# Conditioning bias added by the tensor engine as a 12-row matmul, with the weight, decay-rate and input loads put in another order

## The chip, the cores and the metric

The kernel runs on one core of one Trainium2 chip. The metric is the device time of one execution in microseconds (us), as the median of several runs. TensorE is called PE here, its weight loads PEld, VectorE DVE, ScalarE ACT, GpSimd POOL and SyncE SP. A number such as L939 is a line of the kernel before.

## The reference

One decoder layer for 1024 prompt tokens and 8 single tokens of a decode batch. Only its beginning matters here: the conditioning vector `c` (9 rows: one for the prompt, eight for the samples) goes through one weight of 1024 x 6144, the bias is added, and the first two of six pieces scale and shift the normalised input before the input projection.

```python
def ada_mod(c, w, b):
    m = jax.nn.silu(c) @ w + b
    return m.reshape(c.shape[0], N_MOD, 1, D_MODEL)

def modulate(x, shift, scale):
    return layer_norm(x) * (1.0 + scale) + shift
...
        mp = ada_mod(c_prompt, w_ada[l], b_ada[l])
        ms = ada_mod(c_sample, w_ada[l], b_ada[l])
...
        op, stp = mixer(modulate(xp, mp[:, 0], mp[:, 1]), ...)   # proj = u @ w_in, then two head groups
...
        vp = modulate(xp, mp[:, 3], mp[:, 4])                    # then a top-2 mixture of 32 experts
```

The other pieces of the conditioning are a gate after each sub-layer and the second shift and scale. Behind the projection come a convolution, a recurrence and a scan, an output projection, and a mixture of experts.

## The kernel before

**Stages.** Each engine has its own program, written out by hand in order, and they meet only at semaphores; nothing is scheduled. The first stage (0 to about 73 us) does, on PE: transposes of `c` (L871) and of the eight normalised tiles of x (L885, function `x_turn`), of the eight sample rows (L909) and of small parameter rows (L914, 42 rows; L918, 29 rows). Then the conditioning for shift and scale comes in four pairs, `ada_pair(0)` to `ada_pair(3)`: each is 32 matmuls of a 128 x 32 stationary slice of `c` against a 128 x 128 piece of the weight (L895), four of them side by side in the four column groups of 32, and one transpose (L902). Then the projection begins: `project_split` (L939) runs 72 matmuls for each tile of 128 output columns, eight k slices of nine. For the first tile it waits slice by slice, and takes `ada_pair(2)` and `ada_pair(3)` before slices 2 and 4.

**What DVE and ACT do there.** DVE takes the statistics of each tile of x (L1132, `x_stats`) and normalises it (L1141, `x_norm`), copies the parameter rows out of PSUM (L1158, L1160) and halves some of them (L1161, L1162; PE's `ada_pair(0)` waits for L1162). For a pair it adds the bias (L1176, `u_pair`), copies the transposed result (L1178), applies scale and shift to two slices (L1184), and subtracts for the low part of the split into high and low parts (L1192, `u_low`), after ACT has cast the high part (L721). `w_high` (ACT, L713) and `w_low` (DVE, L1154) do the same for a tile of projection weights. `lam_rates` (DVE, L1100 to L1125) is a chain of 17 small instructions for the decay rates, which are used only much later.

**Late conditioning.** The remaining four pieces are computed between projection tiles: after each of the first eight tiles PE does two k steps, `ada` (L877), each of 4 matmuls with 512 columns, one in each column group. Steps 0 to 7 fill bank 6 of PSUM, steps 8 to 15 bank 7. DVE adds the bias when a bank is full (L1246, `mod_out`).

**Loads.** SP and ACT each issue four of the eight 512 KB tiles of x, even ones on SP behind the two loads of `c`, odd ones on ACT. POOL issues the bias, replicated over partitions in eight DMAs (`bada4` and `badaP`, L513 and L517), then the sample rows and the parameter rows.

Of the kernel before, what the change touches and what calls it, by code (L numbers as in the profile page):

```python
# [25 lines left out]
ALU = mybir.AluOpType  # L26
# [3 lines left out]
P = 128  # L30
# [50 lines left out]
def build_step(nc, x_prompt, x_sample, c_prompt, c_sample, state_lru_conv, state_lru_h, state_ssd_conv,  # L81
# [13 lines left out]
    with ctx:  # L95
# [95 lines left out]
        bada4 = sb("bada4", [P, 3, 512], scope=first)  # L191
        lnst = sb("lnst", [P, 2, 16], scope=first)
# [16 lines left out]
        modP, badaP = at(46300, 4, P), at(43904, 4, P)  # L209
# [71 lines left out]
        bada_ready = sem("bada_ready")  # L281
        sample_ready = sem("sample_ready")
# [104 lines left out]
        with nc.Block() as block:  # L387
            @block.sync
            def _(sp):
# [12 lines left out]
                for t in range(0, NT, 2):  # L402
                    sp.dma_start(xt[t], x_prompt[0, t * P:(t + 1) * P, :]).then_inc(xt_loaded[t], 16)
# [9 lines left out]
                load_pair(2)  # L413
                load_w(COL_XBC + P, 1)
                load_pair(3)
# [87 lines left out]
            def _(gp):  # L503
# [8 lines left out]
                for g in range(4):  # L512
                    gp.dma_start(bada4[32 * g:32 * g + 32, :, :],  # L513
                                 b_ada.rearrange("a (r g n) -> g a r n", r=3, g=4)[g].to_broadcast([32, 3, 512]))\
                        .then_inc(bada_loaded, 16)
                for g in range(4):
                    gp.dma_start(badaP[32 * g:32 * g + 32, :, :],  # L517
                                 b_ada[:, 0:2 * D].rearrange("a (s c i n) -> s i a c n", s=2, c=4, i=2)[g // 2, g % 2]
                                 .to_broadcast([32, 4, P])).then_inc(bada_loaded, 16)
# [8 lines left out]
                for dst, src in ((prow2[0:4, :], ssd_conv_w[0]), (prow2[4:5, :], ssd_conv_b),  # L528
                                 (prow2[5:29, :], state_ssd_conv[0].rearrange("b k n -> (b k) n"))):
                    gp.dma_start(dst, src).then_inc(rows2_loaded, 16)  # L530
                step(gp.memset(ones[:, :], 1.0))
# [126 lines left out]
            def _(act):  # L658
                step = Chain(act, ac)

                for t in range(1, NT, 2):
# [54 lines left out]
                for k in range(KT):  # L716
                    if k == 5:
                        w_high(1, 0)
                    act.wait_ge(u_ready, k + 1)
                    act.wait_ge(sample_ready, k // 2 + 1)  # L720
                    act.activation(us[:, 0, k, :], uT[:, k, :], ACT.Copy).then_inc(uh_ready, 1)  # L721
                act.wait_ge(small_loaded, 64)
# [142 lines left out]
            def _(pe):  # L865
# [8 lines left out]

                def ada(bank, k, w):
                    for g in range(4):
                        mm = pe.matmul(PS[32 * g:32 * g + 32, bank, :], cT[:, k, :], w[:, 512 * g:512 * g + 512],  # L877
                                       start=(k == 0), stop=(k == KT - 1))
                    return mm
# [9 lines left out]
                def ada_pair(c):  # L889
                    pe.wait_ge(pair_loaded[c], 32)  # L890
                    if c > 1:
                        pe.wait_ge(mod0_ready, c - 1)
                    for k in range(KT):
                        for g in range(4):
                            mm = pe.matmul(PS[32 * g:32 * g + 32, 6 + c % 2, 0:P], cT[:, k, :],  # L895
                                           pair[c][g // 2][:, k, P * (g % 2):P * (g % 2) + P],
                                           start=(k == 0), stop=(k == KT - 1))
# [22 lines left out]
                pe.wait_ge(vector_once, PT_READY)  # L920
                ada_pair(0)
# [172 lines left out]
            def _(ve):  # L1094
# [72 lines left out]
                ve.wait_ge(bada_loaded, 128)  # L1167
                step(ve.tensor_scalar(badaP[64:128, :, :], badaP[64:128, :, :], 1.0, None, ALU.add))
                step(ve.tensor_scalar(bada4[0:64, 2, :], bada4[0:64, 2, :], 1.0, None, ALU.add))
# [4 lines left out]
                def u_pair(c):  # L1174
                    ve.wait_ge(ada_mm, c + 1)
                    ve.tensor_tensor(modP[:, c, :], PS[:, 6 + c % 2, 0:P], badaP[:, c, :], ALU.add).then_inc(mod0_ready, 1)  # L1176
# [24 lines left out]
                lam_rates()  # L1201
# [4 lines left out]
                w_low(1, 0)  # L1206
                u_low(6)
                u_low(7)

# [24 lines left out]
                ve.tensor_tensor(wdts[:, 1, :, :], wdt[:, :, :], wdts[:, 0, :, :], ALU.subtract).then_inc(ul_ready, 1)  # L1234

# [1475 lines left out]
```

## Time and profile before

| | |
|---|---|
| median of 3 runs | 1527.1 us (1524.56 to 1530.54) |
| the profiled execution, its own time | 1527.24 us |
| its span in the trace | 1525.3 us |
| PE busy | 1360.6 us, 89% |
| DVE busy | 952.6 us, 62% |
| ACT busy | 572.0 us, 37% |
| POOL busy | 295.9 us, 19% |

The span is the stretch that the trace covers; the execution's own time is 1.9 us longer. Busy time of PE counts overlapping matmuls once, and their ends are modelled, so the start of the next instruction says more than the end of the last. The four parts of the program follow each other: the conditioning and the input (to 73 us), projection, scan and recurrence (to about 620 us), output projection and routing (to 913 us), the experts and the end.

### The profile page before, as it was taken

What the parts mean: (1) busy time and instruction counts of PE and PEld (TensorE: products, weight loads), DVE (VectorE), ACT (ScalarE), POOL (GpSimd) and SP (SyncE); (2) the same over time, 40 slices, a digit from 0 to 9 for tenths busy, and PEclk for the clock granted to TensorE, in tenths of its full rate; (3) what the DMA queues carried; (4) which work ended last, traced back from release to release, by engine and by line L of the source; (5) the groups of instructions that cost most, each with busy time, mean ns of one, the idle gap of its engine ahead of it and who ended that gap; (6) DMA issues with size and microseconds to landing.
All of it is one profiled execution on the core that took longest, in us unless ns stands there. A gap on an engine that the chain in (4) does not pass through costs nothing.

```text
span 1525.3 us, 38250 instructions
## 1 busy us (share of the span) xinstructions
PE 1360.6 (89%) x13487; PEld 1005.5 (66%) x13487; DVE 952.6 (62%) x1702; ACT 572.0 (37%) x886; POOL 295.9 (19%) x325
## 2 busy tenths in 40 slices
PE   4799999999999999789999449998899899999944
PEld 3689989899888888578588435544455455555521
DVE  5755553968999989876777565544444353351639
ACT  3322332535555665722232103433343243241522
POOL 4000002211000000200000013333333343443400
PEclk8899999999999999899999769999999999999977
DMA  9666415644334335832232949999999989978684
GB/s 284 194 241 238 155 42 160 212 147 141 113 113 123 116 113 190 307 96 96 75 99 77 391 161 404 407 406 407 408 407 398 407 349 354 407 290 335 242 334 154
DMA packets 169586, 365.87 MB, mean 240 GB/s; under 512 B 16040, under 2 KB 94944, under 8 KB 166312
## 3 DMA queue, kind: packets, MB, share of 16 engines
q1 hardware_dynamic: 150616, 308.72, 55.2%
q0 software_dynamic: 18320, 54.08, 10.1%
q10 hardware_dynamic: 576, 2.10, 0.4%
q8 instruction: 45, 0.74, 0.2%
q14 instruction: 29, 0.24, 0.0%
HBM read 324.06 MB, written 45.63 MB: 242 GB/s over the span
## 4 chain that ended last, share of the span: by engine, by line
PE 29%; DMA 19%; DVE 7%; issue 2%; SPq 1%; ACT 0%; DVEq 0%; POOLq 0%; ACTq 0%
DMA ring<-in_w_down_dram 18%; PE PS L2069 10%; PE PS L2200 8%; PE PS L2218 5%; DVE big L2270 1%; PE PS L2188 1%; PE PS L2100 1%; DMA ring<-in_w_up_dram 1%; PE PS L2135 1%; PE PS L2209 1%; DVE ring L2647 1%; DVE ring L2652 1%; PE PS L2092 1%; DVE ring L2661 1%; SPq L1678 1%
## 5 line engine op out<-in xcount | busy, mean ns | idle before, releaser
L939 PE MATMUL PS<-big 128*128 128x344 f32 x2592 | 423.0, 323 | 1.7 <-DVE big L1192 1.7
L939 PEld LDWEIGHTS PS<-big 128*128 128x128 f32 x2592 | 411.9, 189 | 10.4 <-issue 6.7
L2200 PE MATMUL PS<-ring,arena 128*32 128x256 f32 x5248 | 301.0, 381 | 0.5 <-DVE arena L2537 0.5
L2200 PEld LDWEIGHTS PS<-ring,arena 128*32 128x32 f32 x5248 | 162.1, 110 | 114.2 <-issue 15.0
L2218 PE MATMUL PS<-ring,arena 128*32 128x256 f32 x2624 | 165.1, 394 | 21.9 <-DVE arena L2545 21.9
L1833 POOL DMA_INDIRECT arena<-v_d,icur x84 | 103.2, 1229 | 281.3 <-DVE icur L2549 159.1
L2000 ACT ACTIVATE ring<-ring 128x1024 f32 x124 | 121.0, 1047 | 58.8 <-PE PS L2200 58.0
L2218 PEld LDWEIGHTS PS<-ring,arena 128*32 128x32 f32 x2624 | 78.7, 112 | 78.4 <-DVE arena L2545 23.7
L1841 POOL DMA_INDIRECT f_d<-arena,scur x82 | 105.8, 1290 | 65.5 <-issue 45.0
L2541 DVE SCALAR_TENSOR_TENSOR arena<-arena,PS 128x128 f32<-128x128 f32 x82 | 23.6, 288 | 138.6 <-ACT arena L1977 93.3
L2592 DVE COPY ring<-ring 128x4096 f32 x31 | 72.7, 2345 | 55.9 <-SPq L1712 41.3
L2537 DVE COPY arena<-PS 128x256 f32<-128x256 f32 x82 | 34.7, 423 | 99.4 <-PE PS L2188 97.8
L1972 ACT ACTIVATE arena<-PS 128x256 f32<-128x256 f32 x82 | 30.7, 374 | 166.5 <-PE PS L2200 166.5
L2069 PE MATMUL PS<-low 128*128 128x512 f32 x256 | 83.3, 407 | 10.9 <-issue 5.0
L1982 ACT ACTIVATE arena<-PS 128x256 f32<-128x256 f32 x82 | 31.4, 383 | 151.0 <-PE PS L2218 151.0
L2579 DVE COPY ring<-ring 128x1024 f32 x124 | 80.3, 688 | 9.2 <-PE PS L2200 3.6
L2069 PE MATMUL PS<-big,low 128*128 128x512 f32 x256 | 81.0, 398 | 0.0
L2069 PE MATMUL PS<-low,big 128*128 128x512 f32 x256 | 80.9, 398 | 0.0
L2069 PEld LDWEIGHTS PS<-low 128*128 128x128 f32 x256 | 47.2, 193 | 22.0 <-issue 8.2
L1154 DVE TENSOR_TENSOR big<-arena,big 128x1024 fp32r<-128x1024 f32 x20 | 24.5, 1225 | 55.4 <-ACT big L713 55.3
L2069 PEld LDWEIGHTS PS<-low,big 128*128 128x128 f32 x256 | 49.3, 193 | 10.9
L2069 PEld LDWEIGHTS PS<-big,low 128*128 128x128 f32 x256 | 49.2, 192 | 10.8
(469 smaller groups left out, 1833.3 us busy)
## 6 DMA issues: line engine op xcount, KB each, us to landing
ring<-in_w_gate_dram SPq DMA_DIRECT2D x32, 2048.0 KB, 10.5
ring<-in_w_up_dram SPq DMA_DIRECT2D x32, 2048.0 KB, 15.6
ring<-in_w_down_dram SPq DMA_DIRECT2D x32, 2048.0 KB, 8.6
arena<-in_w_ada_dram SPq DMA_DIRECT2D x16, 1024.0 KB, 6.8
arena<-in_w_in_dram SPq DMA_DIRECT2D x20, 512.0 KB, 8.0
upper<-in_w_ada_dram SPq DMA_DIRECT2D x8, 1024.0 KB, 11.6
upper<-in_w_in_dram SPq DMA_DIRECT2D x16, 512.0 KB, 4.0
arena<-acs_d SPq DMA_DIRECT2D x8, 1024.0 KB, 4.8
```

Source lines behind the costliest of these rows:

```text
L939: mm = pe.matmul(PS[:, 3 * b + a, 0:CU], wss[b][:, i, k, :], us[:, j, k, a * CU:(a + 1) * CU], start=(k == 0 and (i, j) == PARTS[0]), stop ...
L1833: gp.indirect_dma_start(xg[b], None, v_q, bass.IndirectOffsetOnAxis(ap=icur[b][:, :], axis=0), bounds_check=QW * (SEQ + DEC) - 1, oob_is_e ...
L1841: gp.indirect_dma_start(f_q, bass.IndirectOffsetOnAxis(ap=scur[b][:, :], axis=0), yo[b], None, bounds_check=QW * 2 * (SEQ + DEC) - 1, oob_ ...
L1972: act.activation(hb, PS[:, 3, 0:FH], ACT.Copy).then_inc(hb_ready, 1)
L1982: act.activation(yo[b], PS[:, 6, 0:DQ], ACT.Copy).then_inc(yo_ready, 1)
L2000: act.activation(wcur[:, 1024 * q:1024 * q + 1024], ring[:, bass.ds(w + 1024 * q, 1024)], ACT.Copy).then_inc(gate_copied, 1)
L2069: mm = pe.matmul(PS[:, bank + n, :], (yh[h % 2], yl3[h % 3])[a][:, k, :], (WH, WL)[b][i][:, 512 * n:512 * n + 512], start=(k == 0 and (a, ...
L2200: mm = pe.matmul(PS[32 * g:32 * g + 32, 3, 0:FH], xT[:, c, CAP * q:CAP * q + CAP], wcur[:, w:w + FH], start=(q == 0 and c == 0), stop=(q = ...
L2218: mm = pe.matmul(PS[32 * g:32 * g + 32, 6, 0:DQ], hT[:, c % 2, CAP * (c // 2):CAP * (c // 2) + CAP], wcur[:, 8192 + 1024 * c + DQ * g:8192 ...
L2537: ve.tensor_copy(xT, PS[:, 0, 0:2 * P].rearrange("p (c t) -> p c t", c=2)).then_inc(xT_ready, 1)
L2579: ve.tensor_copy(wcur[:, 4096 + 1024 * q:5120 + 1024 * q], ring[:, bass.ds(w + (4096 + 1024 * q), 1024)]).then_inc(up_copied, 1)
L2592: ve.tensor_copy(wcur[:, GU:GU + DN], ring[:, bass.ds(w, DN)]).then_inc(down_copied, 1)
```

## The change

The bias is loaded once as 12 rows of 512 columns (`brow`, chunk r in partition r), in one DMA in place of eight. POOL builds a column that is 1 in rows 2, 3, 8 and 9 (the two scales) from the identity, and DVE adds it to the 12 rows; PE's first pair now waits for that (`bada_ready`). Each accumulation of the conditioning then begins with a matmul of 12 partitions, whose stationary operand is one column of the identity broadcast to 32 columns, so that it puts row `chunk` of the bias in all 32 output rows. DVE's two additions of the bias become copies. The remaining edits move things: the order of x over the two queues, the second tile of projection weights behind the fourth pair of weights, its cast behind the eight slices on ACT and its subtraction behind them on DVE, and `lam_rates` behind the last of that on DVE.

```diff
-                for t in range(0, NT, 2):
+                for t in (2, 4, 6, 7):
                     sp.dma_start(xt[t], x_prompt[0, t * P:(t + 1) * P, :]).then_inc(xt_loaded[t], 16)
...
                 load_pair(2)
+                load_pair(3)
                 load_w(COL_XBC + P, 1)
-                load_pair(3)
...
-                for g in range(4):
-                    gp.dma_start(bada4[32 * g:32 * g + 32, :, :],
-                                 b_ada.rearrange("a (r g n) -> g a r n", r=3, g=4)[g].to_broadcast([32, 3, 512]))\
-                        .then_inc(bada_loaded, 16)
-                for g in range(4):
-                    gp.dma_start(badaP[32 * g:32 * g + 32, :, :],
-                                 b_ada[:, 0:2 * D].rearrange("a (s c i n) -> s i a c n", s=2, c=4, i=2)[g // 2, g % 2]
-                                 .to_broadcast([32, 4, P])).then_inc(bada_loaded, 16)
+                gp.dma_start(brow, b_ada.rearrange("a (r n) -> (a r) n", n=512)).then_inc(bada_loaded, 16)
...
+                step(gp.tensor_tensor(scale_row[0:NB_ADA, 0:2], ident[0:NB_ADA, 2:4], ident[0:NB_ADA, 8:10], ALU.add))
+                gp.tensor_tensor(scale_row[0:NB_ADA, 2:3], scale_row[0:NB_ADA, 0:1], scale_row[0:NB_ADA, 1:2], ALU.add)\
+                    .then_inc(scale_row_made, 1)
...
-                for t in range(1, NT, 2):
+                for t in (0, 1, 3, 5):
                     act.dma_start(xt[t], x_prompt[0, t * P:(t + 1) * P, :]).then_inc(xt_loaded[t], 16)
...
                 for k in range(KT):
-                    if k == 5:
-                        w_high(1, 0)
                     act.wait_ge(u_ready, k + 1)
                     act.wait_ge(sample_ready, k // 2 + 1)
                     act.activation(us[:, 0, k, :], uT[:, k, :], ACT.Copy).then_inc(uh_ready, 1)
+                w_high(1, 0)
...
+                def bias(out, chunk, lo, n):
+                    pe.matmul(out, ident[0:NB_ADA, chunk:chunk + 1].to_broadcast([NB_ADA, 32]), brow[:, lo:lo + n],
+                              start=True, stop=False)
+
                 def ada(bank, k, w):
                     for g in range(4):
+                        if k == 0:
+                            bias(PS[32 * g:32 * g + 32, bank, :], 4 * (bank - 5) + g, 0, 512)
                         mm = pe.matmul(PS[32 * g:32 * g + 32, bank, :], cT[:, k, :], w[:, 512 * g:512 * g + 512],
-                                       start=(k == 0), stop=(k == KT - 1))
+                                       start=False, stop=(k == KT - 1))
...
+                    for g in range(4):
+                        bias(PS[32 * g:32 * g + 32, 6 + c % 2, 0:P], 2 * (g // 2) + c // 2, 256 * (c % 2) + P * (g % 2), P)
...
                 pe.wait_ge(vector_once, PT_READY)
+                pe.wait_ge(bada_ready, 1)
                 ada_pair(0)
...
-                ve.wait_ge(bada_loaded, 128)
-                step(ve.tensor_scalar(badaP[64:128, :, :], badaP[64:128, :, :], 1.0, None, ALU.add))
-                step(ve.tensor_scalar(bada4[0:64, 2, :], bada4[0:64, 2, :], 1.0, None, ALU.add))
+                ve.wait_ge(bada_loaded, 16)
+                ve.wait_ge(scale_row_made, 1)
+                ve.tensor_scalar(brow, brow, scale_row[0:NB_ADA, 2:3], None, ALU.add).then_inc(bada_ready, 1)
...
-                    ve.tensor_tensor(modP[:, c, :], PS[:, 6 + c % 2, 0:P], badaP[:, c, :], ALU.add).then_inc(mod0_ready, 1)
+                    ve.tensor_copy(modP[:, c, :], PS[:, 6 + c % 2, 0:P]).then_inc(mod0_ready, 1)
...
                 u_low(3)
-                lam_rates()
                 u_pair(2)
                 u_low(4)
                 u_low(5)
                 u_pair(3)
-                w_low(1, 0)
                 u_low(6)
                 u_low(7)
+                w_low(1, 0)
...
                 ve.tensor_tensor(wdts[:, 1, :, :], wdt[:, :, :], wdts[:, 0, :, :], ALU.subtract).then_inc(ul_ready, 1)
+                lam_rates()
...
-                    ve.tensor_tensor(modS[r], PS[:, 5 + r, :], bada4[:, r, :], ALU.add).then_inc(mod_ready, 1)
+                    ve.tensor_copy(modS[r], PS[:, 5 + r, :]).then_inc(mod_ready, 1)
```

On PE, the end of the first projection tile and the two late steps behind it read so before (L939 is the projection, L877 the late step; a row counts matmuls of one kind in a row):

```order
L939 MATMUL PS<-big 128x344 x18
L895 MATMUL PS<-upper 32x128 x32
L902 MATMUL PS<-ident,upper 128x128
L939 MATMUL PS<-big 128x344 x36
L877 MATMUL PS<-arena,upper 32x512 x8
L939 MATMUL PS<-big 128x344 x72
```

and so in the changed kernel, where L948 is the projection, L903 the pair, L876 the bias and L883 the late step:

```order
L948 MATMUL PS<-big 128x344 x18
L876 MATMUL PS<-bada,ident 32x128 x4
L903 MATMUL PS<-upper 32x128 x32
L910 MATMUL PS<-ident,upper 128x128
L948 MATMUL PS<-big 128x344 x36
L876 MATMUL PS<-bada,ident 32x512
L883 MATMUL PS<-arena,upper 32x512
L876 MATMUL PS<-bada,ident 32x512
L883 MATMUL PS<-arena,upper 32x512
L876 MATMUL PS<-bada,ident 32x512
L883 MATMUL PS<-arena,upper 32x512
```

In a pair the four bias matmuls stand together ahead of the 32; in a late bank each of them stands alone, in turn with one matmul of the first k step. The same alternation comes once more, at the first step of the second bank, behind the fifth projection tile.

On DVE, the last two pairs up to the projection loop read so before (L1176 is the bias added to a pair, L1192 `u_low`, L1154 `w_low`, L1100 the beginning of `lam_rates`, which goes on to L1125):

```order
L1100 TENSOR_SCALAR sm<-sm 128x8
...
L1125 TENSOR_SCALAR spl<-sm 128x8
L1176 TENSOR_TENSOR upper<-PS,upper 128x128
...
L1184 TENSOR_SCALAR arena<-arena,ssT 128x1024
L1154 TENSOR_TENSOR big<-arena,big 128x1024
L1192 TENSOR_TENSOR big<-arena,big 128x1032 x2
L1234 TENSOR_TENSOR wdts<-wdt,wdts 128x128
```

and so in the changed kernel (L1185 the copy of a pair, L1201 `u_low`, L1163 `w_low`, L1109 to L1134 `lam_rates`):

```order
L1185 COPY upper<-PS 128x128
...
L1201 TENSOR_TENSOR big<-arena,big 128x1032 x2
L1163 TENSOR_TENSOR big<-arena,big 128x1024
L1242 TENSOR_TENSOR wdts<-wdt,wdts 128x128
L1109 TENSOR_SCALAR sm<-sm 128x8
...
L1134 TENSOR_SCALAR spl<-sm 128x8
```

`lam_rates` has gone from ahead of the third pair to behind everything that the first projection tile needs, and `w_low` from ahead of the last two `u_low` to behind them.

## Rows read from the trace of the kernel before

**Rows 1.** Busy us of each engine in two stretches, then granted PE clock, DMA share, GB/s.

```profile
39.00:54.50 15.50, 12.11 (x148) 10.47 (x148) 10.99 (x21) 5.20 (x6) 0.00 (x0) 0.64 1.10 361
...
130.00:500.00 370.00, 357.69 (x2388) 332.10 (x2388) 270.49 (x432) 160.72 (x235) 36.10 (x50) 1.00 0.44 140
```

**Rows 2.** Timeline at the start, DVE: start, length, instruction, idle before and releaser.

```profile
10.88 1.29 DVE L1132 BATCH_NORM_STATS2 lnst<-arena 128x6 f32<-128x512 f32 x2 [1.88 <-DMA arena<-in_x_prompt_dram]
...
16.30 1.29 DVE L1132 BATCH_NORM_STATS2 lnst<-arena 128x6 f32<-128x512 f32 x2 [1.14 <-DMA arena<-in_x_prompt_dram]
```

**Rows 3.** ACT's tiles of x, issue to landing; then each queue's packets, MB, share.

```profile
L662 ACTq DMA_DIRECT2D arena<-in_x_prompt_dram x4: 395/456/497, 0.9 to 2.3; - x4
...
DMA to landing us min/median/max: 3.9/6.7/9.5
...
q10 hardware_dynamic: 478, 1.76, 42.4%
q1 hardware_dynamic: 239, 0.88, 22.5%
...
q1 hardware_dynamic: 854, 2.40, 38.7%
```

**Rows 4.** Timeline from the parameter rows to the second pair.

```profile
38.95 3.64 PE L895 MATMUL PS<-upper 128*32 128x128 f32 x64 [0.99 <-DVE PT L1162]
...
39.21 0.42 DVE L1168 TENSOR_SCALAR upper<-upper 64x512 f32<-64x512 f32 x1
...
49.75 0.33 PE L902 MATMUL PS<-ident,upper 128*128 128x128 f32 x1 [2.48 <-DVE upper L1176]
```

**Rows 5.** Timeline around the third pair.

```profile
54.50 1.96 PE L895 MATMUL PS<-upper 128*32 128x128 f32 x64
54.95 0.17 DVE L1100 TENSOR_SCALAR sm<-sm 128x8 f32<-128x8 f32 x1
...
58.22 0.29 DVE L1176 TENSOR_TENSOR upper<-PS,upper 128x128 f32<-128x128 f32 x1
```

**Rows 6.** Timeline around the fourth pair and the last slices.

```profile
61.65 1.95 PE L895 MATMUL PS<-upper 128*32 128x128 f32 x64
...
63.36 1.23 DVE L1192 TENSOR_TENSOR big<-arena,big 128x1032 fp32r<-128x1032 f32 x1 [0.67 <-ACT big L721]
64.51 0.28 DVE L1176 TENSOR_TENSOR upper<-PS,upper 128x128 f32<-128x128 f32 x1
...
66.65 2.02 ACT L721 ACTIVATE big<-arena 128x1032 fp32r<-128x1032 f32 x2 [3.32 <-DVE arena L1188]
67.19 1.22 DVE L1154 TENSOR_TENSOR big<-arena,big 128x1024 fp32r<-128x1024 f32 x1
68.33 2.37 DVE L1192 TENSOR_TENSOR big<-arena,big 128x1032 fp32r<-128x1032 f32 x2
...
69.71 3.06 PE L939 MATMUL PS<-big 128*128 128x344 f32 x18 [1.68 <-DVE big L1192]
```

**Rows 7.** Timeline of the first late steps, and what PE and DVE do behind.

```profile
72.70 1.92 PE L877 MATMUL PS<-arena,upper 128*32 128x512 f32 x16
...
73.95 1.23 DVE L1154 TENSOR_TENSOR big<-arena,big 128x1024 fp32r<-128x1024 f32 x1 [3.05 <-ACT big L713]
74.55 11.35 PEld L939 LDWEIGHTS PS<-big 128*128 128x128 f32 x72 [0.84 <-issue]
```

**Rows 8.** PE's groups by shape: busy us, mean ns of one; idle before.

```profile
L877 PE MATMUL PS<-arena,upper 128*32 128x512 f32 x80 | 9.6, 598 | 0.0
```

**Rows 9.** Timeline where PE's shape changes (stationary 8, then 42 partitions), and where not.

```profile
34.53 1.02 PE L909 MATMUL PS<-ident,arena 8*128 8x8 f32 x8
...
35.48 1.08 PE L914 MATMUL PS<-ident,arena 42*128 42x42 f32 x8
...
410.42 1.03 PE L1038 MATMUL PS<-ident,arena 128*128 128x128 f32 x8
411.21 9.08 PE L939 MATMUL PS<-big 128*128 128x344 f32 x56
```

More of the change, by code:

```diff
@@ L191, in build_step @@
         bada4 = sb("bada4", [P, 3, 512], scope=first)
+        scale_row = sb("scale_row", [P, 3], scope=first)
         lnst = sb("lnst", [P, 2, 16], scope=first)
@@ L208, in build_step @@
         modS = [None] + [at(o, 512) for o in (46300, 23176)]
-        modP, badaP = at(46300, 4, P), at(43904, 4, P)
+        modP = at(46300, 4, P)
+        NB_ADA = 12
+        brow = bada4[0:NB_ADA, 0, :]
         xb2 = [at(A0 + 1060 * b, 1060) for b in range(2)]
@@ L281, in build_step @@
         bada_ready = sem("bada_ready")
+        scale_row_made = sem("scale_row_made")
         sample_ready = sem("sample_ready")
@@ L530, in _ @@
                     gp.dma_start(dst, src).then_inc(rows2_loaded, 16)
+                gp.wait_ge(gpsimd_once, IDENT_MADE)
+                step(gp.tensor_tensor(scale_row[0:NB_ADA, 0:2], ident[0:NB_ADA, 2:4], ident[0:NB_ADA, 8:10], ALU.add))
+                gp.tensor_tensor(scale_row[0:NB_ADA, 2:3], scale_row[0:NB_ADA, 0:1], scale_row[0:NB_ADA, 1:2], ALU.add)\
+                    .then_inc(scale_row_made, 1)
                 step(gp.memset(ones[:, :], 1.0))
@@ L896, in ada_pair @@
                                            pair[c][g // 2][:, k, P * (g % 2):P * (g % 2) + P],
-                                           start=(k == 0), stop=(k == KT - 1))
+                                           start=False, stop=(k == KT - 1))
                     mm.then_inc(ada_mm, 1)
```

## The prediction

> **What bounds the kernel now.** I read the windows first. From 130 to 500 us PE is busy for 357.69 of 370 us while DVE has 270 and ACT 161 [rows 1]: behind the first stage the core is bound by PE, and every later stage is started by semaphores that come from there. So an edit to the first 75 us is worth what it does to the moment when PE gets to the second projection tile, and whatever it adds to PE behind that moment counts in full. The timeline of the first stage then shows four places where PE doesn't set the pace:
>
> - DVE's chain of statistics and normalising waits 1.88 us for the first tile of x and 1.14 us for the third [rows 2]; later tiles are there when it comes.
> - `ada_pair(0)` starts at 38.95, released by DVE [rows 4]. It takes 3.64 us for what the third pair does in 1.96 [rows 4, 5]: the granted clock is 0.64 on average from 39 to 54.5 us [rows 1], that is, partly at 1.2 and partly at 2.4 GHz.
> - The third pair ends at 56.46, but DVE takes its result only at 58.22, since the 17 instructions of `lam_rates` stand between (from 54.95) [rows 5].
> - Behind the fourth pair DVE's `w_low` (67.19) stands ahead of `u_low`, which PE's last two slices wait for: 1.68 us at 69.71 [rows 6].
>
> **The change part by part.** A minus sign is a gain.
>
> *Order of x.* ACT's first tile lands 3.9 us after an issue at 0.93, that is at 4.8; its second and third within 6.7 and 9.5 us of issues up to 2.3, by 9.0 and 11.8; SP's first is the one that released DVE at 10.88 [rows 2, 3]. In the new order DVE has tile 0 when it comes, at 9.0 (10.88 less its wait), tile 1 (wanted 1.4 later, at 10.4) from ACT's second slot, and tile 2 (wanted at 16.30 less 1.14 less 1.88 = 13.3) from SP's first. The last ones come on SP in its third and fourth slot; SP's queue has moved 2.40 MB by 22 us, more than the 2.1 MB of its x [rows 3], and they are wanted near 22.6 and 24.9 (tiles follow each other at 2.3 us). So both waits go: **-3.02**. The eight bias DMAs also leave POOL's queue, 1 MB of traffic in the same stretch; I count nothing for it, since nothing is left to wait.
>
> *The 12 rows.* The load, the two POOL instructions and the DMAs behind them are tens of us early. But PE's first pair now also waits for DVE's addition to the 12 rows, which stands where L1168 stood: 39.21, and as long, 0.42 (512 elements per partition in both), so it ends at 39.63. Before, PE began at 38.95, 0.05 or so behind the instruction that released it; now that is 39.68: **+0.73**. Behind PE's wait only the pairs are queued, and DVE has nothing else to do until the first one ends.
>
> *Bias in the pairs.* Four matmuls more per pair are an eighth of a pair: 0.45 at the low clock, 0.25 at the high one. They have 12 partitions where the pair has 128, so PE's shape changes in between. Where the stationary operand goes from 8 to 42 partitions, the next matmul begins 0.07 us before the end of the last (34.53 + 1.02 against 35.48), whereas between two groups of 128 x 128 it begins 0.24 before (410.42 + 1.03 against 411.21) [rows 9]. A change of shape thus loses the overlap of one matmul with the next, 0.17 us at most. I take 0.6 for the first pair and 0.4 for the third and fourth. The second pair ends well ahead of DVE (PE waits 2.48 us behind it [rows 4]): nothing. First pair: **+0.6**.
>
> *lam_rates moved.* DVE can now take the third pair when PE has it, 56.46 + 0.15 = 56.6 in place of 58.22: **-1.6**, and PE's 0.4 is in the path there: **+0.4**. In its new place `lam_rates` fills the 3.05 us in which DVE waits before 73.95 [rows 7]; its 3.3 us may push the next `w_low` by some tenths, but PE needs that one only a tile (11 us) later, so even without the gap it would cost PE nothing until those 11 us were used up.
>
> *w_high and w_low moved.* Without `w_high` in between, ACT has slice 5 cast earlier and DVE loses its wait of 0.67 at 63.36; it could take the fourth pair at 63.84, PE has it at 61.65 + 1.95 + 0.15 = 63.75 plus 0.4 = 64.15, in place of 64.51: **-0.36**. Then `u_low(6)` begins when ACT's first cast is done (66.65 + 1.01, so 67.7) in place of 68.33: **-0.6** for PE's slices 6 and 7 [rows 6]. The moved `w_low` and its load behind `load_pair(3)` are wanted only after the late steps, some 3 us later. The swap on SP's queue brings the fourth pair earlier and the tile later, both with more than 10 us in hand.
>
> Up to the end of the first projection tile: -3.02 + 0.73 + 0.6 - 1.6 + 0.4 - 0.36 - 0.6 = **-3.9**.
>
> *Bias in the late banks.* Here the four bias matmuls aren't together. Each stands between matmuls of 128 partitions, so there are seven changes of shape and seven stretches in which only one column group works, where before four did. A matmul of fp32 is two instructions in the trace (16 for two steps of four). In its 1.92 us [rows 7] there are four rounds of four side by side, so one round streams (1.92 - 0.60) / 3 = 0.44, with 0.60 for one instruction [rows 8]. One matmul by itself: 0.44 + 0.60 - 0.07 (the overlap left at a change) = 0.97. Seven of them, with the eighth overlapping the second step as before: 6.8 us. This falls into PE's own stream, at the end of tile 0 (PE runs from 72.70 to 74.55 without a gap of its own [rows 7]) and again at the end of tile 4. Two banks: **+13.6**.
>
> Here a rule of the Trainium skill bears on the change: TensorEngine Tiling (Array Packing), under Tiling Modes, Key Properties, says that changing the tiling mode, and not just the tile, drains the engine, and lists 32, 64 and 128 rows as modes. The trace agrees (0.07 against 0.24, [rows 9]); by it alone one would get the same 0.97 for each stretch, and without it the first rival below.
>
> DVE's copies in place of additions have the same size and the same single PSUM source; the late one is off the path. Nothing.
>
> **Sum.** -3.9 + 13.6 = +9.7. Against the profiled execution: 1527.24 + 9.7 = 1536.9; the median of the runs is 0.1 lower than that execution, so 1536.8.
>
> **Rivals.**
>
> 1. *The shape doesn't matter: not slower.* If bias matmuls overlap with their neighbours as the four column groups do now, a bank's bias costs two rounds, 0.88, not 6.8, and a pair's 0.45 or 0.25. Then -3.02 + 0.73 + 0.45 - 1.6 + 0.25 - 0.5 - 0.6 + 1.76 = -2.5, 1524.6. For it: the column groups stay the same, and [rows 9] show only groups with other work between semaphores. Against: the overlap left is 0.07 there. It decides below 1.9 us per bank. Chance 0.15.
> 2. *The low clock.* If PE falls to 1.2 GHz in one of the stretches with a single column group (it does twice in the first 55 us), its seven streams of 0.88 double: +6, 1543. For it: less of the array works. Against: by the records PE is hardly idle there, and from 100 us on it stays at full clock [rows 1]. Chance 0.1. The low stretches before 55 us may also shift; the first pair is worth 1.7 us (3.64 against 1.96) either way.
> 3. *x comes later than its slot says.* ACT's queue has moved 1.76 MB by 12 us and SP's 0.88 [rows 3]. Were they even in the new order (1.3 MB each), ACT's second tile would be complete near 10 us and usable 1.5 us after it is wanted: -1.5 in place of -3.0, 1538.3. Chance 0.06. The Trainium skill says in DMA: Bandwidth & Descriptors, Queues, rings and completion order, that each DMA engine serves its queues in turn; the trace doesn't show even shares in this stretch.
> 4. *The delay is taken up later*, by DVE's or the DMA's own waits: some 1530. Against: PE has 12 us of idle time in 370 [rows 1], and what waits for it shifts with it. Chance 0.03.
>
> **How the numbers follow.** The forecast has 0.66, with 1533.5 to 1540.5 as its own range (a tenth of the 0.97 either way is 1.4 us, the first pair's clock 1.7, the x order 1.5). To leave out no more than 2 in 10, the range takes rivals 3 and 4 and most of 2: 1530 to 1543.5; what is left out is above all rival 1. About 0.5% (7.6 us) is what a measurement of this kernel can tell from no change: faster is below 1519.5, for which no case stands, 0.01; slower is above 1534.7, with nearly nine tenths of the forecast and rivals 2 and 3, 0.75; the rest 0.24.
>
> **What would show it.** In the trace of the changed kernel: statistics of the first tile at 9.0 and no wait at the third (x); the first pair near 36.7, released by the addition to the 12 rows; DVE at the third pair at 55.3 in place of 58.22 (`lam_rates`); slice 6 near 65.8; and between the first tile and the second, PE's late steps near 8.7 us long in place of 1.85, with bias and weight matmuls in turn, one per 0.97 us. The second tile's first matmul would then be at 74.55 + 2.9 = 77.5. If the late steps take under 3 us, rival 1 holds and the forecast is wrong; if a single one takes 1.4 us or more, it is the clock.

## The result, and the profile after

The changed kernel takes **1542.24 us** (median of 6 runs, 1538.09 to 1543.38), against 1529.4 us for the kernel before in the same series (6 runs, 1524.56 to 1533.06). The ratio on record is 1.0078, 95% interval 1.0061 to 1.0096: 11.9 us slower (9.3 to 14.7). The two medians differ by 12.8; here and below the ratios on record are used, which differ a little from the quotients of the medians. The profiled execution took 1542.43 us, with a span of 1540.8. The forecast was 1536.8, in a range of 1530 to 1543.5.

PE's timeline of the changed kernel from the last slices of the first projection tile to the start of the second (start, length, instruction, count; idle before and releaser in brackets). It answers to [rows 6] and [rows 7], and its end is the second pass through late steps, at the end of tile 4:

```profile
62.14 3.06 PE L948 MATMUL PS<-big 128*128 128x344 f32 x18 [1.10 <-DVE big L1201]
65.13 1.04 PE L876 MATMUL PS<-bada,ident 12*32 12x512 f32 x2
66.10 1.05 PE L883 MATMUL PS<-arena,upper 128*32 128x512 f32 x2
67.08 1.04 PE L876 MATMUL PS<-bada,ident 12*32 12x512 f32 x2
68.05 1.04 PE L883 MATMUL PS<-arena,upper 128*32 128x512 f32 x2
69.02 1.04 PE L876 MATMUL PS<-bada,ident 12*32 12x512 f32 x2
69.99 1.05 PE L883 MATMUL PS<-arena,upper 128*32 128x512 f32 x2
70.97 1.04 PE L876 MATMUL PS<-bada,ident 12*32 12x512 f32 x2
71.94 1.90 PE L883 MATMUL PS<-arena,upper 128*32 128x512 f32 x10
73.77 4.52 PE L948 MATMUL PS<-big 128*128 128x344 f32 x27
...
125.56 1.04 PE L876 MATMUL PS<-bada,ident 12*32 12x512 f32 x2
...
132.37 1.90 PE L883 MATMUL PS<-arena,upper 128*32 128x512 f32 x10
134.21 11.01 PE L948 MATMUL PS<-big 128*128 128x344 f32 x68
```

The single row of [rows 7] (72.70, 1.92 us, 16 instructions) has become eight rows. None has an idle time in brackets, and still each starts 0.97 us behind the one before. Two steps that took 74.55 - 72.70 = 1.85 us now take 73.77 - 65.13 = 8.64 us, and at tile 4 again 134.21 - 125.56 = 8.65. PE counts as busy all the time: nothing in the chain of waits or in the idle columns shows this loss. It shows in starts that follow each other by 0.97 us, where four matmuls side by side used to stream in 0.44 (the prediction's working from [rows 7] and [rows 8]).

The first stage, where the change moves work, from the timeline of the changed kernel (it answers to [rows 2] and [rows 4 to 6]):

```profile
8.69 1.27 DVE L1141 BATCH_NORM_STATS2 lnst<-arena 128x6 f32<-128x512 f32 x2
...
10.12 1.23 DVE L1141 BATCH_NORM_STATS2 lnst<-arena 128x6 f32<-128x512 f32 x2
...
33.05 0.19 DVE L1171 TENSOR_SCALAR PT<-PT 128x60 f32<-128x60 f32 x1
33.43 0.47 DVE L1178 TENSOR_SCALAR bada<-bada,scale_row 12x512 f32<-12x512 f32 x1
34.00 0.42 PE L876 MATMUL PS<-bada,ident 12*32 12x128 f32 x8 [1.70 <-DVE sm L1174]
34.35 3.21 PE L903 MATMUL PS<-upper 128*32 128x128 f32 x64
...
49.32 0.42 PE L876 MATMUL PS<-bada,ident 12*32 12x128 f32 x8
49.67 1.95 PE L903 MATMUL PS<-upper 128*32 128x128 f32 x64
51.69 0.29 DVE L1185 COPY upper<-PS 128x128 f32<-128x128 f32 x1 [1.85 <-PE PS L903]
...
57.51 0.29 DVE L1185 COPY upper<-PS 128x128 f32<-128x128 f32 x1 [0.21 <-PE PS L903]
```

The first tile of x is met at 8.69 without a wait (before 10.88), and so is the second at 10.12. The addition to the 12 rows ends at 33.90 and PE's first pair starts at 34.00; the releaser that the row names, L1174, had been done 0.5 us before (by DVE's timeline at 33.51). The third pair is taken at 51.69, as soon as PE has it (before 58.22, 1.76 us late). All these moments come earlier than the prediction had them: the first pair at 34.00 (36.7), the third pair at 51.69 (55.3), slice 6 at 62.14 (65.8) and the second projection tile at 73.77 (77.5).

To see where the time comes and goes, the start of each instruction was subtracted from that of the same instruction in the trace of before. This is the difference at several places, in us (negative: earlier than before), for two profiled executions of the changed kernel and, for scale, a second one of the kernel before:

```
at (us, before)        10    17    31    37    43    58    64    71    80   140   240   370   620   905  1200  1520
changed, 1st         -2.2  -3.5  -3.5  -5.4  -5.2  -6.5  -7.0  -7.6  -0.8  +6.0  +6.0 +12.4 +12.7 +14.0 +13.3 +15.5
changed, 2nd         -2.0  -2.4  -2.4  -4.2  -3.1  -4.7  -5.1  -5.7  +1.1  +7.9  +8.3 +10.2 +10.6 +11.8 +11.8 +16.5
before, 2nd          -0.6  -0.9  -0.9  -2.7  -2.7  -2.7  -2.7  -2.7  -2.7  -2.7  -2.7  -2.6  -2.6  -3.3  -3.2  +1.0
```

Three things stand in it. The first stage wins 7.6 us (5.7 in the second execution), not 3.9. Each of the two banks costs 6.8 us in both executions, 13.6 together. And there is a loss that no step of the prediction has: 6.4 us between 240 and 370 us in the first execution, 1.9 in the second (2.3 of it against the shift of 7.9 at 140 us).

### The profile page after: what moved, and what is told of

The parts are those of the page before. It is cut to its first block, busy times and chain, and to the rows that moved or that the text cites. A ratio compares the mean times of both kernels' runs of the same rounds, so it can differ in the third digit from the quotient of the medians.

```text
span 1540.8 us, 38340 instructions
## 1 busy us (share of the span) xinstructions
PE 1387.4 (90%) x13535; PEld 1024.0 (66%) x13535; DVE 953.1 (62%) x1701; ACT 574.7 (37%) x886; POOL 294.7 (19%) x320
## 4 chain that ended last, share of the span: by engine, by line
PE 36%; DMA 11%; DVE 7%; issue 2%; ACT 1%; ACTq 1%; SPq 1%; DVEq 1%; POOLq 0%
PE PS L2209 13%; PE PS L2078 10%; DMA ring<-in_w_down_dram 10%; PE PS L2227 6%; PE PS L2218 1%; PE PS L2197 1%; DVE big L2279 1%; PE PS L2109 1%; PE PS L2144 1%; DVE ring L2656 1%; DVE ring L2661 1%; PE PS L2101 1%; DVE ring L2670 1%; DVE big_end L2291 1%; PE PS L2181 0%
## 5 line engine op out<-in xcount | busy, mean ns | idle before, releaser
L948 PE MATMUL PS<-big 128*128 128x344 f32 x2592 | 428.1, 326 | 1.1 <-DVE big L1201 1.1
L948 PEld LDWEIGHTS PS<-big 128*128 128x128 f32 x2592 | 417.1, 192 | 9.9 <-issue 6.7
L2209 PE MATMUL PS<-ring,arena 128*32 128x256 f32 x5248 | 310.7, 383 | 3.1 <-issue 2.1
L2209 PEld LDWEIGHTS PS<-ring,arena 128*32 128x32 f32 x5248 | 173.7, 110 | 115.6 <-issue 24.6
L2227 PE MATMUL PS<-ring,arena 128*32 128x256 f32 x2624 | 161.6, 386 | 10.0 <-DVE arena L2554 10.0
L1842 POOL DMA_INDIRECT arena<-v_d,icur x84 | 108.2, 1289 | 283.5 <-DVE icur L2558 167.8
L2227 PEld LDWEIGHTS PS<-ring,arena 128*32 128x32 f32 x2624 | 78.6, 110 | 63.5 <-DVE arena L2554 11.5
L2588 DVE COPY ring<-ring 128x1024 f32 x124 | 81.6, 697 | 11.4 <-PE PS L2209 5.8
L1163 DVE TENSOR_TENSOR big<-arena,big 128x1024 fp32r<-128x1024 f32 x20 | 24.5, 1225 | 67.7 <-ACT big L714 67.3
## 6 DMA issues: line engine op xcount, KB each, us to landing
ring<-in_w_gate_dram SPq DMA_DIRECT2D x32, 2048.0 KB, 10.6
upper<-in_w_ada_dram SPq DMA_DIRECT2D x8, 1024.0 KB, 11.9
```

Of the source, the lines that this page charges most:

```text
L948: mm = pe.matmul(PS[:, 3 * b + a, 0:CU], wss[b][:, i, k, :], us[:, j, k, a * CU:(a + 1) * CU], start=(k == 0 and (i, j) == PARTS[0]), stop ...
L1842: gp.indirect_dma_start(xg[b], None, v_q, bass.IndirectOffsetOnAxis(ap=icur[b][:, :], axis=0), bounds_check=QW * (SEQ + DEC) - 1, oob_is_e ...
L2209: mm = pe.matmul(PS[32 * g:32 * g + 32, 3, 0:FH], xT[:, c, CAP * q:CAP * q + CAP], wcur[:, w:w + FH], start=(q == 0 and c == 0), stop=(q = ...
L2227: mm = pe.matmul(PS[32 * g:32 * g + 32, 6, 0:DQ], hT[:, c % 2, CAP * (c // 2):CAP * (c // 2) + CAP], wcur[:, 8192 + 1024 * c + DQ * g:8192 ...
L2588: ve.tensor_copy(wcur[:, 4096 + 1024 * q:5120 + 1024 * q], ring[:, bass.ds(w + (4096 + 1024 * q), 1024)]).then_inc(up_copied, 1)
```

## The experiments

Theory A is the prediction's: a bias matmul has 12 partitions in its stationary operand, the weights have 128, and where the two alternate neither overlaps with the next. Theory B: not the shape but the alternation itself costs (two accumulations interleaved in a bank, or the broadcast operand). Theory C: the loss at 240 to 370 us belongs to where PE's clock is low in an execution, not to the code. Theory D: the moved work causes it.

**All 128 rows, and the four together.** In the first kernel the bias matmul reads all 128 partitions, those behind the 12 rows cleared; order and count stay.

```diff
+        brow_all = bada4[:, 0, :]
...
+                step(gp.memset(brow_all, 0.0))
...
-    pe.matmul(out, ident[0:NB_ADA, chunk:chunk + 1].to_broadcast([NB_ADA, 32]), brow[:, lo:lo + n],
+    pe.matmul(out, ident[:, chunk:chunk + 1].to_broadcast([P, 32]), brow_all[:, lo:lo + n],
```

> The changed kernel, but each bias matmul has 128 partitions (116 of them zero) in place of 12, in the same places and the same alternation. Theory A (a change of PE's shape ends the overlap of neighbouring matmuls): the late steps behind the first tile shrink from 8.6 us to 1.85 + 0.88 = 2.7, and again behind the fifth, so the kernel is about 11.8 us faster than the changed one, near 1530 or a little below the kernel before. Theory B (the alternation itself, two matmuls in turn into the same column group and bank, or the broadcast column, makes PE wait): one matmul per 0.97 us as in the changed kernel, no gain.

The second keeps the 12 partitions, but gives a late bank's four bias matmuls together, ahead of the first step.

```diff
+                    if k == 0:
+                        for g in range(4):
+                            bias(PS[32 * g:32 * g + 32, bank, :], 4 * (bank - 5) + g, 0, 512)
                     for g in range(4):
-                        if k == 0:
-                            bias(PS[32 * g:32 * g + 32, bank, :], 4 * (bank - 5) + g, 0, 512)
```

> The changed kernel, but in a late bank the four bias matmuls of 12 partitions stand together ahead of the first k step. Theory A: two changes of shape per bank in place of eight; the four overlap in the four column groups, so they take 0.97 and perhaps 0.2 more, late steps near 3.0 us in place of 8.6, and the kernel is about 11.4 us faster than the changed one. If matmuls of 12 partitions never overlap (a cost of the bias matmul itself): 4 x 0.97 = 3.9, late steps near 5.8 us, about 5.7 us faster. If it is the accumulation into the same bank that waits: between these.

Medians: 1528.82 us with all rows (ratio 1.0005, 0.9993 to 1.0016) and 1528.62 us grouped (1.0005, 0.9994 to 1.0017), against 1528.08 for before. PE's timeline with all rows:

```profile
68.38 1.08 PE L878 MATMUL PS<-bada,ident 128*32 128x512 f32 x8
69.26 1.92 PE L885 MATMUL PS<-arena,upper 128*32 128x512 f32 x16
71.11 9.10 PE L950 MATMUL PS<-big 128*128 128x344 f32 x56
```

and grouped:

```profile
69.68 1.06 PE L876 MATMUL PS<-bada,ident 12*32 12x512 f32 x8
70.67 1.92 PE L884 MATMUL PS<-arena,upper 128*32 128x512 f32 x16
72.53 7.67 PE L949 MATMUL PS<-big 128*128 128x344 f32 x47
```

The late steps take 71.11 - 68.38 = 2.73 us and 72.53 - 69.68 = 2.85 us, against 8.64. The first kernel issues the same instructions in the same order as the changed one, interleaved and with the broadcast operand: B falls. (The timeline lists its bias and weight matmuls in one row each, since they overlap.) The second has 12 partitions and only two places where the shape changes: the 12-row matmuls overlap with each other. What costs is the number of changes: eight at the late steps of the changed kernel, two here. Each kernel's ratio falls from the changed one's 1.0078 to 1.0005, about 11 us; 11.8 and 11.4 were expected.

**The PE bias alone, and the moves alone.** The first is the kernel before with only the bias of the change (12 rows, matmuls, copies; not all of the lines that go back are shown); the second is the changed kernel with the bias added by DVE as before.

```diff
--- PE bias alone, against the changed kernel
-                for t in (2, 4, 6, 7):
+                for t in range(0, NT, 2):
...
-                load_pair(3)
                 load_w(COL_XBC + P, 1)
+                load_pair(3)
...
+                    if k == 5:
+                        w_high(1, 0)
...
+                lam_rates()
```

> The kernel before with the bias by PE alone: no order of x, weights, casts or decay rates is moved. By the sum: +13.6 for the late banks, +0.7 for the new wait, +0.6 for the first pair, and nothing where DVE is late anyway (lam_rates and w_low still stand there): +15, near 1543 to 1544. A rival, that the bias DMAs (1 MB less traffic) are worth something by themselves because x lands earlier, would make it +12 to +13.

```diff
--- moves alone, against the changed kernel
-                ve.tensor_copy(modP[:, c, :], PS[:, 6 + c % 2, 0:P]).then_inc(mod0_ready, 1)
+                ve.tensor_tensor(modP[:, c, :], PS[:, 6 + c % 2, 0:P], badaP[:, c, :], ALU.add).then_inc(mod0_ready, 1)
```

> The kernel before with all the moves (order of x, second weight tile, casts, subtraction, decay rates) and the bias still added by DVE. By the sum without the bias: -3.0 - 1.6 - 0.8 - 0.6 = -6.0, near 1523. If the 7.6 us that the changed kernel had gained by the end of its first tile are partly a better placed low clock, this may be 7 to 9 in its trace up to the same point. If the 6 us that the changed kernel lost between 243 and 365 us come from the moves, the end is no faster than the kernel before.

The PE bias alone: 1544.64 us, ratio 1.0112 (1.0095 to 1.0129). Its late steps in PE's timeline:

```profile
70.05 1.04 PE L877 MATMUL PS<-bada,ident 12*32 12x512 f32 x2
71.02 1.05 PE L884 MATMUL PS<-arena,upper 128*32 128x512 f32 x2
...
76.86 1.90 PE L884 MATMUL PS<-arena,upper 128*32 128x512 f32 x10
78.69 3.58 PE L949 MATMUL PS<-big 128*128 128x344 f32 x21
```

Again 8.64 us. The moves alone: 1523.57 us, ratio 0.9968 (0.9950 to 0.9985), 4.9 us faster. The two parts, +17.1 and -4.9, make +12.2, and the whole change has +11.9. Moves alone were expected at -6 and PE bias alone at +15, which lies inside the interval of the measurement (14.5 to 19.7). This is the timeline of the moves alone at the third pair; DVE again takes it when PE has it:

```profile
51.94 0.29 DVE L1175 TENSOR_TENSOR upper<-PS,upper 128x128 f32<-128x128 f32 x1 [1.34 <-PE PS L894]
```

**Each move by itself**, in the kernel before: the order of x; `lam_rates` moved; `w_high`, `w_low` and the tile's load moved.

```diff
--- order of x
-                for t in range(0, NT, 2):
+                for t in (2, 4, 6, 7):
...
-                for t in range(1, NT, 2):
+                for t in (0, 1, 3, 5):
--- lam_rates (two places)
-                lam_rates()
...
+                lam_rates()
--- the load, w_high, w_low
+                load_pair(3)
                 load_w(COL_XBC + P, 1)
-                load_pair(3)
...
-                    if k == 5:
-                        w_high(1, 0)
...
+                w_high(1, 0)
...
-                w_low(1, 0)
+                w_low(1, 0)
```

> The kernel before with only the order of x changed. By the sum: -3.0 us, the wait for the first tile (1.88) and the third (1.14) gone in the trace. The run with all moves was 3.2 ahead at 17 us, so the trace should show the same; if the end is not 3 us faster, the gain is lost behind the first stage, to the clock.

> The kernel before with only lam_rates moved behind the first projection tile. By the sum: the third pair is taken 1.6 us earlier, nothing lost later: -1.6. A rival: DVE is late again at the fourth pair or at the last slices, so that less than 1 us is left at the second tile.

> The kernel before with only the second weight tile moved (load, cast, subtraction). By the sum without the bias: the fourth pair 0.7 us earlier, slice 6 another 0.6: -1.3 to -1.4 at the second tile. A rival: the subtraction now comes too late for the second tile, a loss there.

Medians, against 1527.73 for before: 1526.24 us (ratio 0.9992, 0.9979 to 1.0004), 1526.12 (0.9992, 0.9981 to 1.0002) and 1529.03 (1.0006, 0.9991 to 1.0022). No median tells one of them from no change, and added up by their ratios they give -1.5 us where the moves together gave -4.9: with intervals as wide as these the medians show neither the single gains nor that they add up. The traces show the gains in the first stage. In the first the statistics stand at 8.85, as in this row of its timeline:

```profile
8.85 1.27 DVE L1132 BATCH_NORM_STATS2 lnst<-arena 128x6 f32<-128x512 f32 x2
```

At 17 to 31 us it is 3.0 us ahead of the first trace of before and 2.1 ahead of the second. (The two traces below with the old order of x, `lam_rates` moved and the weights' halves moved, stand at -0.9 there, as that second trace does.) With `lam_rates` moved the third pair is met at 55.65 and the shift goes from -0.9 to -2.6 there; with the weights' halves moved it goes from -0.9 to -2.2 between 58 and 71 us. These are the only differences at those places: -1.7 and -1.3.

**Moves, and the bias rows loaded later.** Moves alone, with POOL's eight replicated bias loads given behind the parameter rows (the two loops stand just ahead of the memset of the ones), for what these 1 MB cost the first tiles of x.

> All the moves, the bias added by DVE as before, and POOL's eight bias loads issued behind the parameter rows in place of ahead of them. If the 1 MB of bias is in the way of x at the start, the trace is as far ahead at 17 us as in the changed kernel (3.5 against 3.2 with the moves alone) and the parameter rows come earlier; otherwise no difference to the moves alone, 1523 to 1524. Either way this should be the fastest of the versions, some 4 to 5 us below the kernel before.

1522.25 us, ratio 0.9959 (0.9943 to 0.9976): the fastest here, faster than both kernels, but not to be told from moves alone (0.9968). Its shift at 10 us is -2.0 and at 17 us -3.3, where moves alone have -2.0 and -3.2: with the new order of x the loads cost the first tiles nothing.

**The same kernels again**, one profiled execution each: the changed kernel, moves alone, and the kernel before.

> The changed kernel once more, for a second trace. In the first one it loses 6.4 us against the kernel before between 243 and 365 us, where nothing was changed, and PE's granted clock is at its lower level in four stretches there (in the kernel before in one). Theory C: where the low stretches fall differs from execution to execution, so this trace shows them elsewhere or fewer, and the shift between 243 and 365 us is another (0 to 6). Rival D: the change itself brings them, then they come back at the same work, and the shift is again near 6.

> The kernel with the moves alone once more. Its first trace has the same loss of 6.0 us between 240 and 370 us, without any matmul for the bias. Theory C: another shift this time. Rival D, in the form that the moves bring it: again near 6.

> The kernel before once more. Theory C: it too has low stretches between 240 and 370 us in some executions, so its second trace may be 1 to 6 us later than its first at 370 us. Rival D: one low stretch near 303 us as in the first trace, and the same times within some tenths.

1543.58, 1520.12 and 1527.98 us. The windows of 240 to 370 us (busy us of each engine, then granted PE clock, DMA share, GB/s), first of the changed kernel:

```profile
240.00:370.00 130.00, 123.96 (x758) 120.79 (x758) 85.17 (x115) 45.27 (x97) 27.87 (x38) 0.93 0.53 165
```

the changed kernel again:

```profile
240.00:370.00 130.00, 123.84 (x811) 120.67 (x811) 86.27 (x123) 47.52 (x98) 28.01 (x38) 0.97 0.53 165
```

moves alone:

```profile
240.00:370.00 130.00, 124.49 (x786) 120.75 (x785) 86.62 (x114) 56.52 (x104) 24.97 (x34) 0.95 0.54 170
```

moves alone again:

```profile
240.00:370.00 130.00, 124.74 (x819) 120.99 (x818) 92.99 (x135) 58.09 (x109) 25.55 (x35) 0.99 0.55 176
```

and the kernel before:

```profile
240.00:370.00 130.00, 124.53 (x814) 120.80 (x814) 91.44 (x135) 55.50 (x105) 29.02 (x39) 0.99 0.59 185
```

PE is busy for 124 us in all five, but does fewer instructions where the clock is lower (758 against 814). How far each kernel falls behind the first trace of before from 240 to 370 us, beside this clock:

```
                          clock   us lost
changed, 1st               0.93      6.4
moves alone, 1st           0.95      6.0
moves, late bias load      0.95      5.9
grouped bias               0.97      3.5
changed, 2nd               0.97      1.9
all rows                   0.98      1.9
PE bias alone              0.99      0.9
before, 2nd                0.99      0.1
moves alone, 2nd           0.99     -0.3
```

The three kernels with a single move (order of x, `lam_rates`, weights' halves) lose 1.5, 2.0 and 1.7 us, at 0.99, 0.98 and 0.98. The columns are not to be read to the last tenth. In the second execution of the changed kernel, with all rows and with grouped bias the low clock begins just where the stretch does, and against the shift of 140 us they lose 2.3, 2.3 and 4.1. In the first trace of moves alone a part of the low clock lies ahead of the window (0.85 from 226 to 236 us), since this kernel is 7.6 us further on.

The same code loses 6.4 or 1.9 us, and 6.0 or nothing; PE bias alone, which has the two banks in full, loses 0.9. As a fixed cost of the moved work D falls, and C holds: where the loss is large, the clock is low. That the moves make low clock more likely isn't ruled out: all losses above 2.5 us are in kernels with all the moves (four of their seven traces), none in the five other traces. The three repeats also ran on another chip than the experiments, by the record, so they don't tell an execution's share from the chip's. The twelve executions of moves alone, all on one chip, do: they range from 1515.37 us at a mean granted clock of 0.955 to 1527.70 at 0.948. Against before's 0.99 a clock of 0.93 leaves out 0.06 x 130 = 7.8 us of full-speed time (an estimate), against 6.4 measured.

## Why the prediction was right, and where it was not

**The late banks: right in mechanism and size.** The 0.97 us per matmul, worked out as one round's streaming plus its own length less the overlap left, is the step in the rows above to the hundredth; seven of them per bank are 6.8 us, and 13.6 for two. The overlap of 0.07 was read where the clock was at its low level (0.50 from 31 to 38 us, see below) and set against 0.24 at the high one; the changed kernel has 0.07 at the high level too (65.13 + 1.04 against 66.10), so it didn't matter. All rows in use takes it away, grouping takes it away, PE bias alone brings it: this cause is shown. Rival 1 (the shape doesn't matter) is false, and so is rival 2: no matmul of these steps takes 1.4 us. The Trainium skill says in TensorEngine Tiling (Array Packing), Tiling Modes, Key Properties, that a change of tiling mode drains the engine. The all-rows kernel agrees: only the row extent differs, and the late steps take 2.73 us in place of 8.64.

**The time: in the range, in part by luck.** 1542.24 lies outside the 1533.5 to 1540.5 that the prediction gave its own mechanism. It lies inside 1530 to 1543.5 because the range was stretched for rival 2, which didn't happen. Of the 5.4 us above the forecast 2.3 are the kernel before's, which measured 1529.4 here and 1527.1 then. In the first trace a first stage 3.7 us better than forecast stands against losses behind it (9.5 us from 240 us to the end) that the prediction doesn't have.

**The first stage: -7.6 (second execution -5.7) in place of -3.9.** Its steps:

- *Order of x, forecast -3.02.* Measured -3.5 (changed kernel, at 17 us), -3.0 by itself; against the second trace of before -2.1. The first trace of before was late by 0.6 us at the first tile by itself, and the term carried that. Rival 3 (ACT's second tile comes late) is false: the second tile is met at 10.12 without a wait.
- *The bias DMAs, forecast nothing.* In the old order of x it seems not to be nothing: in its one trace PE bias alone meets the third tile at 14.57 without a wait, where three traces with the eight bias loads (before again, `lam_rates`, weights' halves) have 15.39, 15.24 and 15.43, so 0.7 to 0.9 us; but the first trace of before is as far from these three. In the new order it is nothing (-3.3 against -3.2 above), and there the step holds.
- *The wait for 12 rows, forecast +0.73.* Without it PE would start some 0.06 behind L1171, at 33.3; it starts at 34.00: +0.7.
- *Bias in the first pair, forecast +0.6.* Bias and pair take 34.35 + 3.21 - 34.00 = 3.56 us, against 3.64 before [rows 4]: the bias matmuls add 0.35 (34.35 - 34.00), at the high clock here, and less low clock in the pair gave it back. In the second execution both are at the low level, as the term had it (granted clock 0.50 from 33 to 39 us), and there the bias adds 0.58 and bias and pair take 36.06 + 3.59 - 35.48 = 4.17 us, 0.53 more than before: the size holds. These are its rows:

```profile
35.48 0.65 PE L876 MATMUL PS<-bada,ident 12*32 12x128 f32 x8 [1.70 <-DVE sm L1174]
36.06 3.59 PE L903 MATMUL PS<-upper 128*32 128x128 f32 x64
```

- *Bias in the later pairs +0.4, `lam_rates` -1.6.* 0.35 (49.67 - 49.32) and -1.7.
- *`w_high` and `w_low`, forecast -0.96.* -1.3 by themselves, and -1.1 in the changed kernel (58 to 71 us), with the fourth pair's bias in it.
- *The clock*, which rival 2 only mentioned. Between 31 and 37 us, at the transposes of the parameter rows, the changed kernel gains 1.9 us, and a second execution of the unchanged kernel gains 1.8.

This is the window of 31 to 38 us, of the changed kernel:

```profile
31.00:38.00 7.00, 4.86 (x92) 4.07 (x90) 2.07 (x8) 2.74 (x4) 0.00 (x0) 0.78 1.09 349
```

of the kernel before:

```profile
31.00:38.00 7.00, 6.64 (x43) 5.67 (x41) 2.88 (x7) 3.63 (x4) 0.14 (x2) 0.50 1.11 346
```

and of its second execution:

```profile
31.00:38.00 7.00, 5.47 (x73) 4.75 (x74) 4.18 (x12) 4.65 (x6) 0.14 (x2) 0.73 1.10 347
```

0.50 is 1.2 GHz throughout. The first trace of before, on which every term was made, had the low level over the whole stretch; the sum of -3.9 was thus against an unfavourable start, and some 2 us of the -7.6 are not the change's. Such a start isn't rare: of the thirteen traces at hand six have 0.50 in this window (the first of before, all rows, grouped, `lam_rates`, weights' halves, late bias load), and all rows and grouped, otherwise the changed kernel up to here, gain nothing between 31 and 37 us. By differences of traces the order of x gives 2.1 to 3.0, `lam_rates` 1.7 and the weights' halves 1.1, with the fourth pair's bias: 4.9 to 5.8 us, less 1.4 for the PE bias (the wait, the first and the third pair), so -3.5 to -4.4. The forecast of -3.9 stands within that; the traces' totals have the clock in them.

**Behind 240 us: the term that is missing.** The prediction took the clock to be full from 100 us on and made no term for its falling there. [rows 1] don't show that: they cover 130 to 500 us, and a mean over 370 us rounds a short low stretch away; in the same trace the clock is 0.84 from 296 to 306 us, and 0.89 from 620 to 913 us. In the first trace of the changed kernel the loss from 240 to 370 us was 6.4 us, and it is the larger part of why that trace ends at +15.5 although the steps give -7.6 + 13.6 = +6.0. Rival 4 (the delay is taken up later) is false: in none of the three traces with the two banks in full does it get smaller between 140 and 370 us. What decides where PE's clock falls wasn't found. The windows of 266 to 276 us, of the changed kernel:

```profile
266.00:276.00 10.00, 10.00 (x56) 9.97 (x56) 1.79 (x3) 4.19 (x10) 3.59 (x5) 0.83 0.80 288
```

and of the changed kernel again:

```profile
266.00:276.00 10.00, 10.00 (x69) 9.76 (x68) 0.29 (x1) 3.82 (x10) 3.60 (x5) 1.00 0.76 285
```

PE is busy for all 10 us in both, and only in the first is it partly at the lower level. Another 3 to 6 us between 620 us and the end (+12.7 to +15.5 and +10.6 to +16.5 in the changed kernel, but also -2.6 to +1.0 in before's second execution) is left open as well.

Moves alone gained 7.6 and 7.7 us at 71 us in both executions, and only 4.9 in the median: one of its traces gives 6.0 back between 240 and 370 us, and the other doesn't. The profiled executions aren't typical of their kernels either: that of PE bias alone (1540.87 us) is the fastest of its five and that of the order of x (1522.44) of its twelve, while that of the late bias load (1529.63) is the slowest.

So +11.9 against the forecast of +9.7: 13.6 for the banks and -3.5 to -4.4 for the first stage leave 2 to 3 us. That these are the clock's is argued from the traces and not shown: the interval of the measurement is as wide. One thing speaks against mere noise: the same sum leaves 2 to 3 us in each of the kernels with the bias on PE. With all rows and grouped it gives -1.5 to -2.6 (1.8 and 2.0 for the banks) against +0.8 measured, and for PE bias alone 13.8 to 14.7 against +17.1, while for moves alone it gives -5.1 to -6.0 against -4.9. A further cost of the PE bias behind the first stage isn't ruled out, and stays open.

## What to carry to other kernels

Where matmuls in different column groups run side by side, keep the partition count of the stationary operand the same throughout such a stream (here 12 stood between 128s; other counts weren't tried): pad it with zeros, or group the odd ones. At a change of shape a matmul no longer runs beside its neighbour (here each then starts 0.97 us behind the last), and the profile shows it as busy time and not as a wait. Adding a bias by matmul isn't free. Here PE sets the end behind the first stage, and DVE is hardly relieved: its copy of a pair takes 0.29 us (51.69), as its addition did (58.22 in [rows 5]). Even the cheap forms (0.9 to 1.0 us per bank) were no faster than before, while the moves with DVE's addition were. And before a few us in a trace are put down to code, look at a second trace of the same kernel: this one differs from itself by 2 to 6 us at places.

## What was not expected of the hardware

- Stretches of low clock come back while PE is busy without a gap, and not at the same places in two traces of one kernel (granted clock 0.93 and 0.97, and 0.95 and 0.99, over 240 to 370 us). In the first trace of the changed kernel PE is busy for all of 226 to 306 us, and the clock is 0.83 from 246 to 256 and from 266 to 276.
- Four bias matmuls with 12 partitions, side by side, cost 0.99 us (70.67 - 69.68) and with 128 partitions 0.88 (69.26 - 68.38): fewer rows save nothing, and here a change of shape costs 0.11.
